# Vector makes the sums and low parts that GpSimd made, and the last norm moves to the second feed-forward turn, in a two-layer hybrid encoder step

## The reference

```python
    mix = jnp.concatenate([o_mla, o_hg, o_gla], axis=-1) @ lp['w_o']
    x = x + g1 * mix

    h2 = rmsnorm(x, lp['norm_ffn']) * (1.0 + sc2) + sh2
    a, u = jnp.split(h2 @ lp['w_ffn_in'], 2, axis=-1)
    x = x + g2 * ((jax.nn.silu(a) * u) @ lp['w_ffn_out'])
```

## Time and profile before

| | before |
|---|---|
| median of 3 runs | 3300.82 us |
| the profiled execution | 3316.22 us, span 3314.4 us |
| granted TensorE clock, mean | 0.981 |
| PE busy | 3100.8 us (94%) |
| DVE busy | 2221.8 us (67%) |
| ACT busy | 1427.0 us (43%) |
| POOL busy | 1594.5 us (48%) |

### The profile page before, as it was taken

The page is one execution under the profiler, slowest core; times in us unless marked ns, Lnnn a source line. Parts: engine busy times, 40 slices in busy tenths (PEclk is TensorE's granted clock), DMA queues, the critical chain, the costliest instruction groups (busy, mean ns, idle before and its releaser), DMA issues. The chain is left out here.

```text
span 3314.4 us, 61734 instructions
## 1 busy us (share of the span) xinstructions
PE 3100.8 (94%) x21870; PEld 2778.7 (84%) x21870; DVE 2221.8 (67%) x3553; ACT 1427.0 (43%) x3199; POOL 1594.5 (48%) x1627
## 2 busy tenths in 40 slices
PE   6999999999899998999989999898998999989999
PEld 5997666768889998999989966666698999989999
DVE  5312556655688888888872045665647888888886
ACT  5222345444454444444452233454434544444444
POOL 2213566520556566666521145664216565665663
PEclk8999999999999999999999999999999999999999
DMA  6415711113023232222233272110211222222222
GB/s 218 140 69 186 241 44 59 36 36 125 7 84 102 89 101 77 90 76 102 75 109 116 78 227 77 54 52 29 98 52 51 77 102 89 78 92 98 76 101 93
DMA packets 241007, 306.93 MB, mean 93 GB/s; under 512 B 19705, under 2 KB 206414, under 8 KB 240814
## 3 DMA queue, kind: packets, MB, share of 16 engines
q1 hardware_dynamic: 185900, 227.65, 21.0%
q10 hardware_dynamic: 44354, 45.25, 4.3%
q0 software_dynamic: 10560, 31.44, 2.6%
HBM read 264.74 MB, written 39.56 MB: 92 GB/s over the span
## 5 line engine op out<-in xcount | busy, mean ns | idle before, releaser
L1938 PE MATMUL banks<-act_split,w_sets_first 128*128 128x272 f32 x4224 | 561.3, 292 | 33.1 <-issue 13.2
L1938 PEld LDWEIGHTS banks<-act_split,w_sets_first 128*128 128x128 f32 x4224 | 548.2, 191 | 38.0 <-issue 19.6
L1938 PE MATMUL banks<-hidden_split,w_out_split 128*128 128x272 f32 x4224 | 542.6, 289 | 8.3 <-DVE x L3313 5.4
L1938 PEld LDWEIGHTS banks<-hidden_split,w_out_split 128*128 128x128 f32 x4224 | 535.0, 189 | 10.2 <-DVE x L3313 6.9
L1938 PE MATMUL banks<-act_split,w_sets_last 128*128 128x272 f32 x3168 | 427.4, 291 | 38.9 <-DVE product_sums L3297 22.1
L1938 PEld LDWEIGHTS banks<-act_split,w_sets_last 128*128 128x128 f32 x3168 | 406.8, 189 | 52.1 <-DVE product_sums L3297 24.6
L3313 DVE SCALAR_TENSOR_TENSOR x<-banks,mod,x 128x272 f32<-128x272 f32 (+1 forms) x880 | 337.1, 433 | 45.1 <-PE banks L1938 43.8
L1938 PE MATMUL banks<-act_split,w_split 128*128 128x384 f32 (+1 forms) x2016 | 344.9, 331 | 11.0 <-DVE act_split L2731 10.8
L1938 PEld LDWEIGHTS banks<-act_split,w_split 128*128 128x128 f32 x2016 | 337.7, 191 | 15.5 <-issue 10.4
L1938 PE MATMUL banks<-w_split_tm,act_split 128*128 128x396 f32 (+1 forms) x1728 | 317.2, 344 | 0.0
L1938 PEld LDWEIGHTS banks<-w_split_tm,act_split 128*128 128x128 f32 (+1 forms) x1728 | 300.9, 182 | 13.2 <-issue 4.0
(11 more groups left out here) (285 smaller groups left out, 5481.3 us busy)
## 6 DMA issues: line engine op xcount, KB each, us to landing
w_raw<-in_w_ffn_in SPq DMA_DIRECT2D x88, 1024.0 KB, 5.1
w_raw<-in_w_ffn_out SPq DMA_DIRECT2D x44, 1024.0 KB, 5.0
w_mod_front<-in_w_mod ACTq DMA_DIRECT2D x50, 512.0 KB, 5.8
w_mod_third<-in_w_mod ACTq DMA_DIRECT2D x26, 512.0 KB, 5.4
z_token_major<-z_stage POOLq DMA_DIRECT2D x64, 198.0 KB, 2.2
r_qkg<-z_feature_major SPq DMA_DIRECT2D x16, 576.0 KB, 4.3
r_v<-z_token_major SPq DMA_DIRECT2D x16, 512.0 KB, 3.6
w_raw<-in_w_o SPq DMA_DIRECT2D x8, 1024.0 KB, 6.5
```

The source lines that it names most:

```text
L1938: return T.matmul(out, lhsT, rhs, start=start, stop=stop, skip_group_check=True)
```

## The change

Four things are edited, the same way in both layers:

- The low parts `l5` and `l6` of both weight halves move from POOL to DVE, in every turn. SP's waits for the raw weights change with them.
- The activation sums T1, T2, T3 move from POOL (`h_step`) to DVE (`h_add`, which also makes T4), in both passes. T4 of the second pass moves up from behind `x10` to behind `x4`.
- The norm of the last token chunk (8 squares on ACT, 7 additions on POOL) moves from the end of the projection to the second turn, T1; its column sum and root move to T2.
- The pieces of the second pass move from T1 and T2 to T3 and T4, and the loop begins at T5.

```diff
@@ POOL @@
-                    for name in ("l5", "l6"):
-                        w_step("u", g, name)
-                    hook("l6")
+                    hook("sums")
...
-                    if not last:
-                        for name in ("l5", "l6"):
-                            w_step("a", g + 1, name)
...
-                for q in range(19):
+                for q in (0, 1, 2, 3, *range(6, 18)):
                     add(q)
...
+                def adds_at(name):
+                    return {"S2": (1,), "m11u": (2,), "sums": (3, 4), "m22u": (5,), "m12u": (6,), "end": (7,)}[name]
...
+                group(g0)
+                group(g0 + 1, last_adds)
@@ ACT @@
+                def squares(name):
+                    at = ("p1a", "s11a", "s22a", "g11", "u2u", "g21", "g22", "g12")
+                    if name in at:
+                        last_square(at.index(name))
...
-                    if name in ("u3a", "g11", "g22", "end"):
-                        h_high(1, {"u3a": "B11", "g11": "B21", "g22": "T1", "end": "T2"}[name])
+                    if name in ("u3a", "g11", "u2u", "s21a"):
+                        h_high(1, {"u3a": "B11", "g11": "B21", "u2u": "T1", "s21a": "T2"}[name])
...
                 group(g0, first)
-                group(g0 + 1, pieces_of(0))
-                group(g0 + 2, pieces_of(4))
-                with act.Fori(3, NGROUP - 1) as i:
+                group(g0 + 1, squares)
+                group(g0 + 2, rooted)
+                group(g0 + 3, pieces_of(0))
+                group(g0 + 4, pieces_of(4))
+                with act.Fori(5, NGROUP - 1) as i:
@@ SP @@
-                    wait(sp, "fwa_dve", turn - 1, "l4")
-                    wait(sp, "fwa_pool", turn - 1, "l6")
+                    wait(sp, "fwa_dve", turn - 1, "l5")
@@ PE @@
-                        wait(pe, f"fw{b}_pool" if i >= 5 else f"fw{b}_dve", g, f"l{i}")
+                        wait(pe, f"fw{b}_dve", g, f"l{i}")
@@ DVE @@
+                h_add(0, "T1")
+                h_add(0, "T2")
                 project(19)
...
                     w_low("u", g, 4)
+                    w_low("u", g, 6)
                     hidden("11", 0)
                     out_low(g, 3)
                     if not last:
                         w_low("a", g + 1, 0)
+                    hook("a0")
+                    w_low("u", g, 5)
+                    summed("c22u", 2, 2, 5, ("ffn_act", g, "u3u"))
+                    if not last:
                         w_low("a", g + 1, 3)
-                    summed("c22u", 2, 2, 5, ("ffn_act", g, "u3u"))
...
-                        if not last and q in (5, 8):
-                            w_low("a", g + 1, {5: 2, 8: 4}[q])
+                        if not last and q in (5, 8) or q in lows:
+                            w_low("a", g + 1, {5: 2, 8: 4, 10: 6, 13: 5}[q])
...
-                    if name == "c11u":
+                    if name == "h11":
+                        h_add(1, "T1")
+                    elif name == "a0":
+                        h_add(1, "T2")
+                    elif name == "c12a":
                         h_low(1, "B11")
-                    elif name == "x9":
+                    elif name == "h12":
                         h_low(1, "T1")
-                    elif name == "x10":
-                        h_fourth(1)
-                    elif name == "x12":
+                    elif name == "x4":
+                        h_add(1, "T4")
+                    elif name == "x7":
                         h_low(1, "B21")
-                    elif name == "x14":
+                    elif name == "x11":
                         h_low(1, "T2")
```

More of the change, by code:

```diff
@@ new lines, in adds_at, with last_adds @@
+                def adds_at(name):
+                    return {"S2": (1,), "m11u": (2,), "sums": (3, 4), "m22u": (5,), "m12u": (6,), "end": (7,)}[name]
+                def last_adds(name):
+                    s = st("n2_pool")
+                    cn = CHUNKS[2][1]
+                    for d in adds_at(name):
+                        wait(pool, "n2_act", l, f"sq2_{d}")
+                        if d > 1:
+                            wait(pool, "n2_pool", l, f"ad2_{d - 1}")
+                        s.done(V.tensor_tensor(ACC1[:, 2, 0:cn], ACC1[:, 2, 0:cn], SQ[:, d % 2, 0:cn], ALU.add), f"ad2_{d}")
@@ L1127, in next_adds @@
                 def next_adds(name):
                     if l + 1 < DEPTH:
-                        for d in {"S2": (1,), "m11u": (2,), "l6": (3, 4), "m22u": (5,), "m12u": (6,), "end": (7,)}[name]:
+                        for d in adds_at(name):
                             norm_add(l + 1, 0, d)
-                group(g0, first)
-                for i in range(1, 3):
+                group(g0)
+                group(g0 + 1, last_adds)
+                for i in range(2, 5):
                     group(g0 + i)
-                with pool.Fori(3, NGROUP - 1) as i:
+                with pool.Fori(5, NGROUP - 1) as i:
@@ L1824, in group, with last_square @@
                     hook("end")
+                def last_square(d):
+                    s = st("n2_act")
+                    c0, cn = CHUNKS[2]
+                    out = SQ[:, d % 2, 0:cn] if d else ACC1[:, 2, 0:cn]
+                    if not d:
+                        wait(act, "hs_dve", 2 * l, "lB22")
+                        wait(act, "wo_dve", l, "o23")
+                    elif d >= 3:
+                        wait(act, "n2_pool", l, f"ad2_{d - 2}")
+                    s.done(S.activation(out, X[:, d, c0:c0 + cn], ACT.Square), f"sq2_{d}")
                 g0 = 2 * l * NGROUP
-                for q in range(6):
+                for q in range(4):
                     square(q)
@@ L3238, in h_low @@
                     wait(dve, "hs_act", turn, name)
-                    if name == "T1" or name == "B11" and p == 0:
-                        wait(dve, "hs_pool", turn, "T1" if name == "B11" else "T2")
-                    elif name in ("T2", "T4") or name == "B21" and p == 0:
-                        own("hs_dve", turn, "T4")
+                    if name in ("T1", "T2", "T3", "T4"):
+                        own("hs_dve", turn, name)
                     src = h_sum(name) if name[0] == "T" else h_source(name, p)
```

155 lines of the change are left out of this document (67 added, 88 removed).

## The result

The changed kernel takes 3277.33 us (median of five runs, 3272.84 to 3279.46) against 3304.9 (3299.5 to 3313.44) for the kernel before, run beside it: ratio 0.9906, 95% interval 0.9887 to 0.9926. Measured again in a later comparison it was 0.9911 (0.9893 to 0.9930). So the change is a gain of 0.9%, clear of the noise. The prediction was 3274, range 3254 to 3298.

What follows compares the result with a forecast made beforehand. PE, busy 94% of the span, was taken as the bound, its waits to be won. Terms -14.9 - 13 + 3.7 + 0 - 2.9 = -27.1 took the profiled 3316.2 to 3289; the runs' median, 15.4 lower, gave 3274 us, range 3254 to 3298.

Steps and rivals of the forecast that it cites:

- Part 1: Repeated turns, l5 and l6 on DVE: 3u stops waiting, 4u about 0.2 late; 0.55 us per turn, 14.9 in all.
- Part 2: The start, T0 in both layers: 1a, 2a and 7a start earlier; gain 6.5 us per layer, 13 in all.
- the 1.1 charged for the clock: T0 behind 7a's wait of 5.5 us: PE at the lower clock level, 1.1 us more.
- Part 3: T1 to T4 in both layers, with the moved norm and pieces: 2.0 us more per layer, +3.7 in all.
- Part 4: T10 and T11: 79.3 us counted, 80.8 taken as the lower clock may come; no change, bounds -4 and +5 per layer.
- Part 5: T12 of the first layer: without l5 and l6 on POOL, 36.9 us in place of 39.76, gain 2.9.
- B: Rival, chance 0.18: everything freed is kept, 0.75 per repeated turn, T0 8.6 per layer, T10 and T11 -3; 3257 us.
- C: Rival, chance 0.10: in repeated turns the wait only changes its name, 4u waiting as long as 3u did; 3289 us.
- D: Rival, chance 0.07: one more POOL instruction ahead of l5 of u on DVE makes 4u 1.3 late; slower, 3314 us.
- E: Rival, chance 0.05: DVE's long rows stay, so POOL's relief is without worth; as C at T0's lower bound, 3295 us.

Runs made afterwards that it cites:

- e2: The changed kernel with the low part a3 ahead of c22u on DVE again; 3283.3 us in a single run.
- e1: The kernel before with one line moved, the low part a3 behind c22u on DVE; 3285.1 us, ratio 0.9937.
- e4: The changed kernel with l5 and l6 of both weight sets back on POOL; 3279.9 us, ratio 0.9923.
- e5: The changed kernel with the last columns' norm back at the projection's end and in T0, pieces in turns T1 and T2; 3283.2 us in a single run.
- e8: The changed kernel with, in T10 alone, ACT's high parts of sums T1, T2 behind u3u and s12a, DVE's sum T2 behind c22u; 3278.2 us, single run.
- e6: The changed kernel with one more 128x272 tensor_tensor on POOL in T13 to T20 of the second layer; 3282.9 us in a single run.

## Why the prediction was right, and where not

**The sum.** Forecast -27.1; the medians give 3277.3 - 3304.9 = -27.6 in the first comparison. That it came within half a us is luck: the interval of the ratio is 13 us wide, and the terms below missed by 4.1, 1.6 and 0.4 to the one side (parts 2, 4, 3) and by 1.0 and 0.9 to the other (parts 1, 5). The two profiled spans lie 39.5 apart (3314.4 and 3274.9); the stages below give -31, and the other 8 lie in stages whose order the change leaves alone.

**Part 1, repeated turns.** Right by mechanism and nearly by size: 34.05 to 33.54, 0.51 where 0.55 was forecast; with 13 turns in each layer and T12 of the second, -13.9 for -14.9. DVE's rows came as counted: from the start of `l4` on, `l6`, `h11`, POOL's S2, `out_low(3)`, `a0`, `l5` and `c22u` all end within 0.05 us of the times in the prediction. 4u started 0.26 late for the 0.2 forecast, and its products took 0.10 longer. That `l5` and `l6` on DVE are enough for this gain is shown by e2, 0.51 with `a3` in its old place. What the step did not see is that they aren't needed for it: with `a3` moved alone the gain is 0.68 (e1), and with both low parts back on POOL 0.69 (e4).

**Part 2, T0.** The biggest miss in size: -8.2 and -8.9 per layer (first, second) with the start wait, where -6.5 was taken with bounds 4 and 9. 2a's stall went from 6.62 to 0.83, 1a's from 1.58 to nothing, and 7a's wait grew to 4.89. Counted in the second layer from the projection's last block, 7a starts 7.1 earlier where 6.0 was counted, and from 7a to T1 it takes 27.9 where 28.0 was counted without the clock. So half of the miss is 7a's earlier start, and the other half the 1.1 charged for the clock: the products of 7a took 3.06, but they had taken 2.87 before, so the lower level cost hardly more than it already had. Most of the gain is the norm's move (e5), which the step had inside "POOL has only its four weight sums" without a number of its own.

**Part 3, T1 to T4.** +1.4 and +1.9 per layer, less than the 2.0 of the step. T1 is 36.50 (forecast 36.4), but 4u starts 2.7 late and not 3.2, by waits of 1.3 at 4u, 0.6 at 6u and small delays between; the output part adds 0.6. T3 36.9 in place of 37.3. That the move "costs in T1 what its pieces cost less in T0" is wrong: it costs 3.2 in T1 to T4 and wins 5.5 and 6.5 at T0 (e5).

**Part 4, T10 and T11.** No change was forecast; -1.1 and -0.5. 4u in T10 started 4.2 late as forecast (1262.34 - 1240.03 = 22.31 for twelve products of 1.51), in a wait of 0.64 ahead of 4a and one of 3.13 ahead of 4u. The two turns took 79.7 and 80.2 (first, second layer), nearer to the 79.3 that the step had counted than to the 80.8 that it took with 1.5 for the clock: T11's first five products took 7.80 and not 10.52. The two waits named there, 4u's and `h21`'s, come from the same DVE row: e8 took the first away and the second grew.

**Part 5, T12.** -2.0 for -2.9. 4u starts 3.1 late (3.3 forecast), with waits of 1.50 there and 0.73 at 6u; the output part takes 1.4 longer, 0.8 of it a wait for an `x`, which the step left out.

**The rivals.** B was right for T0 alone, which kept 8.5 of its 8.6 per layer; the repeated turns kept 0.51 of its 0.75, T10 and T11 0.8 of its 3 per layer. C's condition, 4u as late as 3u had been, didn't come: 0.26 of 0.75. D's mechanism is shown by e6, at 0.59 per turn for a 272 wide instruction. The weight sums that D meant, 512 wide, weren't tried; their 1.1 stays an estimate. E is refuted by DVE's rows of 0.68; its own sum, C with 5 us less at T0, gives 3294 and not 3295.

## What to carry to other kernels

Before work is moved from one engine to another, look at what stands ahead of the late instruction on its own engine and is not needed before it: one line moved brought two thirds of what the whole change did (0.63% of 0.94%), and the next such line 0.36 us in every repeated turn. The work that was moved between the engines took away the same wait, for 0.51 us a turn in place of 0.68. A wait removed on PE is worth something only if the engine that feeds it has idle time between there and PE's next wait (DVE in T10 had none). And when a step is moved later, ask which load is issued behind it: the last reader of a buffer carries the load of the next turn, and here PE waited 4.5 us for it at once.
